# Expert retrieval of a two-layer decoder on one core: selection of pairs in calls of four heads over 64 candidates, tile 2's keys chosen within the up pass, gate groups from tile 53

## The chip, the cores and the metric

The kernel runs on 1 core of one Trainium2 chip. Its time is the device time of one execution in microseconds (us), the median over runs. TensorE is written PE, its weight load PEld, VectorE DVE, ScalarE ACT, GpSimd POOL, and SyncE, which only issues transfers here, SP.

## The reference, cut to what matters

The model is one step of a decoder with two layers, for 512 prompt tokens and 64 sample tokens. Each layer ends with a channel mixer (PEER) that is nearly all of the time:

```
def peer(xn, wq, subkeys, u, v):                      # 8 heads, 16 of 128 x 128 experts a head
    q = (xt @ wq).reshape(t, 8, 2, 128)
    s = einsum('thpc,pnc->thpn', q, subkeys)          # 2 x 128 scores a head
    sv, si = top_k(s, 16)
    cand = sv[:, :, 0, :, None] + sv[:, :, 1, None, :]      # 16 x 16 sums
    cv, ci = top_k(cand.reshape(t, 8, 256), 16)
    ia, ib = si[..0..][ci // 16], si[..1..][ci % 16];  eidx = ia * 128 + ib
    gate = softmax(cv)
    hc = gelu(einsum('chkd,cd->chk', u[eidx], x), approximate=False)
    return einsum('chk,chkd->cd', hc * gate, v[eidx])
```

Since both lists of 16 are sorted, a sum at place (i, j) can be among the 16 largest only if (i+1)(j+1) is at most 16. 50 of the 256 places are such.

## The kernel before, in words

The 576 tokens are four tiles of 128 prompt tokens (0 to 3) and 64 sample tokens. The mixer treats them in two ways. **Dense:** for the 384 tokens of tiles 0 to 2 every one of the 16384 experts is computed, 128 experts at a time: the *up pass* of 128 expert tiles `m` (`up(m)`: 24 matmuls of 128x384, results through Gelu to HBM), then the *down pass* of 128 tiles (`down(n)`), where the hidden values are weighed with a gate matrix that is zero for experts not chosen. The gate matrix is made during the up pass, four tokens at a time (a *group*, 96 a layer): DVE makes one-hot vectors (`one_hots`, tiles hotA and hotB), ACT weighs them (`weigh_ones`), PE multiplies them (`gates`), ACT copies the result (`copy_gates`), and eight groups are stored in one 2 MB transfer. **Sparse:** for the 64 sample tokens and tile 3 the chosen rows of `u` and `v` are gathered from HBM by POOL, 128 rows of 4 KB at once (`gather(k)`, 192 gathers of `u` a layer), and DVE forms a dot product of each (`dots`, tiles rowsA and rowsB, a ring of 8 slots: gather k waits for dot k-8).

Matmuls in float32 are done in three passes on a rounded half and a rest: ACT makes `high` of each expert tile (`high_tile`), POOL makes `low` (L490), PE needs both.

Ahead of the up pass, PE projects 16 query tiles (`project_tile`) and scores each against the keys (`scores(j)`, j = 0 to 15: head j//2, side j%2), ACT copies the scores (`copy_scores`), and DVE selects. `stage1(l, j)` takes the 16 best of 128 keys for four token tiles (`max`, `max_index`, `match_replace`, `max`, `max_index`). `stage1_samples` does the same for the samples, `best_pairs` selects 16 pairs from 16 x 16 sums and looks up their two indices with one-hot compares, products and sums of 16 x 16 elements a pair list. It is called for one head at a time of tile 3 (`last_tile_pairs`, 8 calls) and of the samples (`sample_pairs`, 4 calls of two heads folded on the partitions) while the queries are made, and for eight heads of tiles 0 to 2 (`dense_pairs`) during the up pass. The gathers wait for `picked`, which follows the sparse selections.

All order is written by hand, and every engine executes its list in order. Three schedules tie the engines together by the expert tile m of the up pass:

- POOL issues `low(m)` and then gathers until `gathers_by(m)` of them are issued, so `low(m+1)` stands behind the gathers of m.
- ACT, after the Gelu of tile m, executes `weigh_ones` of the groups of tile m+1, `copy_gates` of the groups of m, and then `high_tile(m + 3)`. `groups_of(m)` is set by GROUP0 (first tile with a group) and GROUPS_PER_TILE.
- DVE executes the three `dense_pairs` with 20 dots in each, then the dots up to 64, then `one_hots`: before group g stand 64 + 7/5 g dots (two after each of two groups in five, one after the others). DVE can be at most six groups ahead of PE.

Of the kernel before, what the change touches and what calls it, by code (L numbers as in the profile page):

```python
# [25 lines left out]
P = 128  # L26
# [26 lines left out]

C_ID, C_IOTA, C_FOLD = 0, P, 2 * P
# [42 lines left out]
EXP_S, EXP_T = 8, (14, 26, 39)  # L97
TURN_T = (28, 41, 52)
GROUP0, GROUPS_PER_TILE = 45, 1.25
# [13 lines left out]
def gathers_by(m):  # L113

    if m < 4:
        n = 0
    elif m < 6:
        n = 4 * (m - 3)
    elif m < GROUP0:
        n = 8 + 1.55 * (m - 5)  # L120
    else:
        n = 70 + 1.7 * (m - GROUP0)
    return min(int(n), DOTS_UP + 3)
# [6 lines left out]
    "sc_read": 2 * PH, "scS_read": PH // 2, "ss_done": PH // 2, "ex_in": PH + PH // 2 + ND, "ex_out": 2 + ND, "turned": ND, "slot_ready": ND, "slots": ND,  # L130
# [43 lines left out]
def decoder(nc, xin, consts, params, wts, wv, stconv, kcT, kc, vc, uT, u, v,  # L174
            yT, convP, hOut, kNew, vNewP, vNewS, kKeep, vKeep, convS, gate_dram, s_dram):
    with ExitStack() as ctx:
# [90 lines left out]
        cabf = st.take("cabf", [P, 2, PH, TOPK])  # L267
# [9 lines left out]
        sc = st.take("sc", [P, 6, 4, KEYS])  # L277
        sc2 = st.take("sc2", [P, 4, KEYS])
        scS2 = st.take("scS2", [P, 2, KEYS])
        qT = st.take("qT", [P, 6, T])  # L280
        st = Span(nc, gblk_at, SB_HI)
# [224 lines left out]
        def _(act):  # L506
# [70 lines left out]
            def queries(l):  # L577
                d0 = (D_PQ0, D_PQ1)[l]

                def copy_scores(j):  # L580
                    act.wait_ge(sem("sc_done"), after("sc_done", l, j + 1))
                    if j >= 6:
                        act.wait_ge(sem("sc_read"), after("sc_read", l, j - 5))
                    act.activation(sc[:, j % 6].rearrange("p t k -> p (t k)"), ps[:, 4 + j % 2, :], ACT.Copy
                                   ).then_inc(sem("sc_copied"), 1)
# [27 lines left out]
            def hidden(l):  # L613
# [34 lines left out]
                for m in range(KEYS):  # L648
# [119 lines left out]
        def _(dve):  # L768
# [125 lines left out]
            def stage1(l, j):  # L894

                b = sc[:, j % 6]
                dve.wait_ge(sem("sc_copied"), after("sc_copied", l, j + 1))
                for t in range(4):
                    chain.did(dve.max(sv[:, t, j, 0:8], b[:, t]))
                chain.settle()  # L900
                for t in range(4):
                    chain.did(dve.max_index(si[:, t, j, 0:8], sv[:, t, j, 0:8], b[:, t]))  # L902
                    chain.did(dve.match_replace(sc2[:, t], sv[:, t, j, 0:8], b[:, t], BIG))
                chain.settle()
                for t in range(4):
                    ins = dve.max(sv[:, t, j, 8:16], sc2[:, t])
                    if t < 3:
                        chain.did(ins)
                ins.then_inc(sem("sc_read"), 1)
                chain.settle()  # L910
                dve.wait_ge(sem("sc_read"), after("sc_read", l, j + 1))
                for t in range(4):
                    chain.did(dve.max_index(si[:, t, j, 8:16], sv[:, t, j, 8:16], sc2[:, t]))  # L913
# [22 lines left out]
            def experts(l):  # L936
# [36 lines left out]
                def best_pairs(svt, sit, nh, g, ex, ia, ib, free=None, between=None):  # L973


                    c, c2 = cand[:, 0:nh], cand2[:, 0:nh]
# [5 lines left out]
                    chain.did(dve.tensor_tensor(  # L982
                        c.rearrange("p h (i j) -> p h i j", i=TOPK),
                        s4[:, :, 0].unsqueeze(3).broadcast_to([P, nh, TOPK, TOPK]),
                        sb.unsqueeze(2).broadcast_to([P, nh, TOPK, TOPK]), ALU.add))
# [28 lines left out]
                    chain.did(dve.tensor_scalar(cab[:, 0, 0:nh], ci[:, 0:nh], 4, None, ALU.logical_shift_right))  # L1014
                    chain.did(dve.tensor_scalar(cab[:, 1, 0:nh], ci[:, 0:nh], TOPK - 1, None, ALU.bitwise_and))
# [6 lines left out]
                    eq = [b_.rearrange("p h (k i) -> p h k i", k=TOPK) for b_ in (c, c2)]  # L1022
# [294 lines left out]
        def _(pe):  # L1317
# [42 lines left out]
            def experts(l):  # L1360
                w0, d0 = (W_PQ0, W_PQ1)[l], (D_PQ0, D_PQ1)[l]

                def scores(j):
# [4 lines left out]
                    for t in range(4):  # L1368
                        ins = pe.matmul(ps[:, 4 + j % 2, t * KEYS:(t + 1) * KEYS], qT[:, j % 6, t * P:(t + 1) * P], sk,
# [314 lines left out]
```

## Time and profile before

| | |
|---|---|
| median of 3 runs | 3456.17 us (3449.89 to 3461.92) |
| the profiled execution | 3455.42 us, its span 3453.6 us |
| busy: PE, PEld, DVE, ACT, POOL | 89%, 81%, 75%, 40%, 47% of the span |
| DMA | 927 MB, 268 GB/s over the span |
| chain that ended last | PE 61%, DVE 25%, DMA 8% |

A layer's mixer goes through the query stage (from 299 us in layer 0, from 2039 us in layer 1), the up pass (to 1125 and 2864 us) and the down pass (538 us each). The share of an engine says little here, for the three stages have different limits; windows and the steps of one tile tell more. A busy PE is modelled: it counts as busy when its matmuls are merely stretched.

### The profile page before, as it was taken

How to read it: one execution, taken by the hardware profiler on the slowest of the kernel's cores; microseconds unless marked ns; L12 is line 12 of the kernel's file. 1: busy time of each engine (PE TensorE's matmuls, PEld its weight loads, DVE VectorE, ACT ScalarE, POOL GpSimd, SP SyncE). 2: the span in 40 equal slices, each digit the busy share in tenths (PEclk: the TensorE clock that was granted, in tenths of full speed). 3: DMA queues.
4: the chain of work that ended last, by engine and by line, in shares of the span. 5: the costliest groups of instructions: out<-in, count | busy, mean ns of one | idle time of the engine just before them, and what ended most of it. 6: DMA issues, size and time to landing. Idle time of an engine off the chain costs nothing.

```text
span 3453.6 us, 46653 instructions
## 1 busy us (share of the span) xinstructions
PE 3077.7 (89%) x17142; PEld 2786.4 (81%) x17142; DVE 2603.6 (75%) x5039; ACT 1373.3 (40%) x2513; POOL 1620.5 (47%) x1157
## 2 busy tenths in 40 slices
PE   6865959999999899999787789499999998999996
PEld 5765959999999688888684679499999997888885
DVE  3745999976653799999657349899766646999997
ACT  2312214466665233333334222144666653333332
POOL 3441239877776234333230032299777763333340
PEclk9977979999999999999897799799999999999998
DMA  3354239999998999999220022299999989999993
GB/s 96 97 26 56 65 127 362 349 360 374 343 347 307 377 412 404 412 410 406 99 74 18 7 61 63 87 344 361 369 359 367 337 311 381 409 405 411 409 410 129
DMA packets 297411, 927.21 MB, mean 268 GB/s; under 512 B 36640, under 2 KB 86560, under 8 KB 293392
## 3 DMA queue, kind: packets, MB, share of 16 engines
q1 hardware_dynamic: 164016, 418.78, 35.2%
q0 software_dynamic: 111280, 404.77, 31.0%
q10 hardware_dynamic: 21888, 100.67, 7.2%
q8 instruction: 137, 2.24, 0.3%
q14 instruction: 90, 0.74, 0.1%
HBM read 820.48 MB, written 105.53 MB: 268 GB/s over the span
## 4 chain that ended last, share of the span: by engine, by line
PE 61%; DVE 25%; DMA 8%; issue 2%; ACT 2%; POOL 2%; SPq 0%; DVEq 0%; ACTq 0%; POOLq 0%
PE ps L1442 31%; PE ps L1390 14%; PE ps L1340 8%; PE ps L1422 4%; DMA rowsB<-u,pick 3%; DVE rowsB L959 2%; DVE rowsA L959 2%; POOL low L490 1%; DMA hOut<-hlast 1%; DMA sring<-s_dram 1%; DVE cand L1024 1%; DVE cand L1031 1%; DVE si L913 1%; DVE si L902 1%; DMA rowsA<-u,pick 1%
## 5 line engine op out<-in xcount | busy, mean ns | idle before, releaser
L611 ACT ACTIVATE high<-raw 128x1024 fp32r<-128x1024 f32 x512 | 541.9, 1058 | 918.4 <-PE ps L1442 686.6
L1390 PE MATMUL ps<-xh,high 128*128 128x384 f32 x2048 | 706.7, 345 | 60.3 <-POOL low L490 60.1
L490 POOL TENSOR_TENSOR low<-raw,high 128x1024 fp32r<-128x1024 f32 x256 | 613.8, 2398 | 255.6 <-ACT high L611 252.7
L1390 PE MATMUL ps<-xh,low 128*128 128x384 f32 x2048 | 690.6, 337 | 0.0
L1390 PE MATMUL ps<-xl,high 128*128 128x384 f32 x2048 | 689.7, 337 | 0.0
L1442 PE MATMUL ps<-high,hh 128*128 128x512 f32 x1536 | 483.8, 395 | 27.0 <-DVE low L1103 27.0
L1442 PE MATMUL ps<-low,hh 128*128 128x512 f32 x1536 | 482.0, 395 | 0.0
L1442 PE MATMUL ps<-high,hl 128*128 128x512 f32 x1536 | 480.7, 394 | 0.0
L1390 PEld LDWEIGHTS ps<-xh,high 128*128 128x128 f32 x2048 | 389.2, 190 | 68.3 <-POOL low L490 66.5
L1390 PEld LDWEIGHTS ps<-xl,high 128*128 128x128 f32 x2048 | 389.3, 190 | 0.0
L1390 PEld LDWEIGHTS ps<-xh,low 128*128 128x128 f32 x2048 | 388.0, 189 | 0.0
L481 POOL DMA_INDIRECT rowsB<-v,pick x192 | 200.2, 1043 | 365.2 <-DVE ps L966 313.7
L959 DVE SCALAR_TENSOR_TENSOR rowsB<-rowsB,ps 128x1024 f32<-128x1024 f32 x192 | 232.4, 1214 | 182.3 <-DMA rowsB<-u,pick 181.7
L1442 PEld LDWEIGHTS ps<-high,hh 128*128 128x128 f32 x1536 | 288.7, 188 | 95.5 <-DVE low L1103 27.7
L481 POOL DMA_INDIRECT rowsA<-v,pick x192 | 196.6, 1024 | 318.3 <-DVE ps L966 312.2
L1442 PEld LDWEIGHTS ps<-low,hh 128*128 128x128 f32 x1536 | 288.4, 188 | 70.9
L1442 PEld LDWEIGHTS ps<-high,hl 128*128 128x128 f32 x1536 | 289.0, 188 | 69.3
L1340 PE MATMUL ps<-xh,high 128*128 128x288 f32 x1184 | 266.9, 308 | 81.6 <-DVE xl L788 81.5
L959 DVE SCALAR_TENSOR_TENSOR rowsA<-rowsA,ps 128x1024 f32<-128x1024 f32 x192 | 231.9, 1213 | 107.9 <-DMA rowsA<-u,pick 107.2
L1103 DVE TENSOR_TENSOR low<-raw,high 128x1024 fp32r<-128x1024 f32 x256 | 311.6, 1217 | 0.0
L630 ACT ACTIVATE hotB<-hotB,slotT 128x128 f32<-128x128 f32 x768 | 242.0, 390 | 76.3 <-DVE hotB L1078 75.9
L653 ACT ACTIVATE sring<-ps 128x384 f32<-128x384 f32 x256 | 124.7, 487 | 367.6 <-PE ps L1390 366.5
(234 smaller groups left out, 5190.0 us busy)
## 6 DMA issues: line engine op xcount, KB each, us to landing
raw<-uT SPq DMA_DIRECT2D x256, 512.0 KB, 6.9
raw<-v SPq DMA_DIRECT2D x256, 512.0 KB, 10.3
s_dram<-sring ACTq DMA_DIRECT2D x128, 384.0 KB, 7.1
gate_dram<-gblk ACTq DMA_DIRECT2D x24, 2048.0 KB, 11.1
gt<-gate_dram SPq DMA_DIRECT2D x32, 1536.0 KB, 15.8
sring<-s_dram SPq DMA_DIRECT2D x128, 384.0 KB, 10.6
raw<-wts SPq DMA_DIRECT2D x76, 512.0 KB, 3.6
rowsB<-u,pick POOLq DMA_INDIRECT x192, 8.2
```

Source lines behind the costliest of these rows:

```text
L481: pool.indirect_dma_start(out=row_slot(k), out_offset=None, in_=u if k < S0 + S1 else v, in_offset=bass.IndirectOffsetOnAxis(ap=pick[:, c: ...
L490: pool.tensor_tensor(low[:, m % 4], raw[:, m % 4], high[:, (m + 2) % 3].bitcast(F32), ALU.subtract).then_inc(sem("lo_ready"), 1)
L611: act.activation(high[:, (m + 2) % 3], tile_raw(m), ACT.Copy).then_inc(sem("hi_ready"), 1)
L630: ins = act.activation(hotB[:, k], hotB[:, k], ACT.Copy, scale=slotT[:, 2, n:n + 1])
L653: act.activation(sring[:, p % 4, m % 2], ps[:, m % 2, 0:DN], ACT.Gelu).then_inc(sem("g_up"), 1)
L902: chain.did(dve.max_index(si[:, t, j, 0:8], sv[:, t, j, 0:8], b[:, t]))
L959: dve.scalar_tensor_tensor(row, row, 1.0, wide(XS0 if k < S0 else XS1), ALU.mult, ALU.mult, accum_out=phid[:, c:c + 1]).then_inc(sem("row_ ...
L1103: dve.tensor_tensor(tile_low(m), tile_raw(m), high[:, (m + 2) % 3].bitcast(F32), ALU.subtract).then_inc(sem("vlo_ready"), 1)
L1340: ins = pe.matmul(ps[:, 2 * i + h, 0:H2], a[:, c], x[:, c, h * H2:(h + 1) * H2], start=(c == 0 and j == 0), stop=(c == NC - 1 and j == 2))
L1390: ins = pe.matmul(ps[:, m % 2, 0:DN], w[:, c], x[:, c, 0:DN], start=(c == 0 and k == 0), stop=(c == NC - 1 and k == 2))
L1422: ins = pe.matmul(ps[:, 2 + g % 2, i * P:(i + 1) * P], hotB[:, k], hotA[:, k], start=True, stop=True)
L1442: ins = pe.matmul(ps[:, YC[c] + d, :], h[:, n % 3, c * P:(c + 1) * P], w[:, d * 512:(d + 1) * 512], start=(n == 0 and i == 0), stop=(n == ...
```

## The change

It has four parts. (1) `best_pairs` forms only 64 sums (rows of 16, three of 8, four of 4, eight of 1: PAIR_ROWS) instead of 256, scans 64 elements, and turns the place in the list of 64 into i and j with a chain of 14 small instructions. It is called for four heads at once: twice for tile 3 and once for the samples. (2) `stage1` treats token tiles 0, 1 and 3 only. Tile 2's scores are kept (scL) and selected by `stage1_late` between `dense_pairs(1)` and `dense_pairs(2)`, 16 lists in four lots, each lot followed by two dots. The ring of score copies is 4 deep instead of 6. (3) `gathers_by` starts at tile 7 instead of 4, and runs at 1.45 a tile instead of 1.55, then at 1.95 instead of 1.7. (4) Groups begin at tile 53 instead of 45, at 1.4 a tile instead of 1.25. Exponentials and transposes of the slots move to later tiles.

```diff
-EXP_S, EXP_T = 8, (14, 26, 39)
-TURN_T = (28, 41, 52)
-GROUP0, GROUPS_PER_TILE = 45, 1.25
+EXP_S, EXP_T = 12, (22, 34, 54)
+TURN_T = (32, 52, 66)
+GROUP0, GROUPS_PER_TILE = 53, 1.4
+SCR = 4
+EARLY, LATE = (0, 1, 3), 2
...
 def gathers_by(m):
-    if m < 4:
+    if m < 7:
         n = 0
-    elif m < 6:
-        n = 4 * (m - 3)
+    elif m < 9:
+        n = 4 * (m - 6)
     elif m < GROUP0:
-        n = 8 + 1.55 * (m - 5)
+        n = 8 + 1.45 * (m - 8)
     else:
-        n = 70 + 1.7 * (m - GROUP0)
+        n = 74 + 1.95 * (m - GROUP0)
     return min(int(n), DOTS_UP + 3)
...
+            def stage1_late(js):
+                chain.settle()
+                for j in js:
+                    chain.did(dve.max(sv[:, LATE, j, 0:8], scL[:, j]))
...
                 def best_pairs(svt, sit, nh, g, ex, ia, ib, free=None, between=None):
-                    c, c2 = cand[:, 0:nh], cand2[:, 0:nh]
+                    c, c2 = cand[:, 0:nh, 0:PAIRS], cand2[:, 0:nh, 0:PAIRS]
...
-                    for a in range(2):
-                        chain.did(dve.tensor_copy(cabf[:, a, 0:nh], cab[:, a, 0:nh]))
+                    chain.did(dve.tensor_copy(i_, cab[:, 0, 0:nh]))
+                    chain.did(dve.tensor_copy(j_, cab[:, 1, 0:nh]))
+                    chain.settle()
+                    dots(g)
+                    chain.did(dve.tensor_scalar(i_, i_, -1.0, 0.0, ALU.add, ALU.max))
+                    chain.settle()
+                    chain.did(dve.scalar_tensor_tensor(i_, j_, -6.0, i_, ALU.add, ALU.max))
...
                 for j in range(2 * PH):
                     stage1(l, j)
-                    if j % 2:
-                        chain.settle()
-                        last_tile_pairs(j // 2)
                     if j % 4 == 0 and j:
-                        sample_pairs(j // 4 - 1)
-                sample_pairs(PH // 2 - 1)
+                        stage1_samples(l, j // 4 - 1)
+                    if j == PH:
+                        last_tile_pairs(0)
+                stage1_samples(l, PH // 2 - 1)
+                sample_pairs()
                 take_rows(0, S0, slot[:, 0, 0, 0:S0], slot[:, 0, 1, 0:S0])
+                last_tile_pairs(1)
                 take_rows(S0, S1, slot[:, 1, 0], slot[:, 1, 1])
                 dense_pairs(0, normalise_sparse)
                 dense_pairs(1, lambda: normalise_dense(0))
+                for q in range(4):
+                    stage1_late(range(4 * q, 4 * q + 4))
+                    dots(2)
                 dense_pairs(2, lambda: normalise_dense(1))
```

On DVE, in `best_pairs` for eight heads of a dense tile, the piece from the last scans to the first one-hot compare was this before (cab and cabf hold the split place, the row with rowsA or rowsB is a dot):

```order
L1010 MAX_INDEX ci_101<-cv_100,cand2_105 128x8 x2
L959 SCALAR_TENSOR_TENSOR rowsA_118,phid_89<-rowsA_118,ps 128x1024
L1014 TENSOR_SCALAR cab_102<-ci_101 128x128
L1015 TENSOR_SCALAR cab_102<-ci_101 128x128
L1018 CAST cabf_103<-cab_102 128x128 x2
L1024 TENSOR_TENSOR cand_104<-cabf_103,ps 128x2048
```

and is this in the changed kernel:

```order
L1043 TENSOR_SCALAR cab_102<-ci_101 128x128
L1044 TENSOR_SCALAR cab_102<-ci_101 128x128
L1045 CAST cabf_103<-ci_101 128x128
L1047 CAST cabf_103<-cab_102 128x128
L1048 CAST cabf_103<-cab_102 128x128
L982 SCALAR_TENSOR_TENSOR rowsA_119,phid_89<-rowsA_119,ps 128x1024
L1051 TENSOR_SCALAR cabf_103<-cabf_103 128x128
L1053 SCALAR_TENSOR_TENSOR cabf_103<-cabf_103 128x128
L1055 SCALAR_TENSOR_TENSOR cabf_103<-cabf_103 128x128
L1057 TENSOR_SCALAR cabf_103<-cabf_103 128x128
L1058 TENSOR_SCALAR cabf_103<-cabf_103 128x128
L1060 SCALAR_TENSOR_TENSOR cabf_103<-cabf_103 128x128
```

Four small instructions became fourteen (two TENSOR_TENSOR follow the rows shown after one more SCALAR_TENSOR_TENSOR), nearly all with SBUF operands alone, and one dot stands between them: a dense call holds 21 dots instead of 20.

On DVE, at the first gate group, the list before was (the x4 row is `dots(S0 - rows_done)`; 64 dots stand ahead of the first hotA):

```order
L1037 TENSOR_REDUCE slot_94<-cand2_105 128x128
L959 SCALAR_TENSOR_TENSOR rowsB_88,phid_89<-rowsB_88,ps 128x1024
L959 SCALAR_TENSOR_TENSOR rowsA_118,phid_89<-rowsA_118,ps 128x1024 x4
L1078 TENSOR_TENSOR hotA_107<-ps,slotT_93 128x512
L1078 TENSOR_TENSOR hotB_108<-ps,slotT_93 128x512
L959 SCALAR_TENSOR_TENSOR rowsB_88,phid_89<-rowsB_88,ps 128x1024 x2
```

and is now:

```order
L1084 TENSOR_REDUCE slot_94<-cand2_105 128x128
L982 SCALAR_TENSOR_TENSOR rowsA_119,phid_89<-rowsA_119,ps 128x1024
L1125 TENSOR_TENSOR hotA_107<-ps,slotT_93 128x512
L1125 TENSOR_TENSOR hotB_108<-ps,slotT_93 128x512
L982 SCALAR_TENSOR_TENSOR rowsA_119,phid_89<-rowsA_119,ps 128x1024
L982 SCALAR_TENSOR_TENSOR rowsB_88,phid_89<-rowsB_88,ps 128x1024
```

71 dots (3 x 21 + 8) stand ahead of the first group now. On POOL, from the low half of tile 44, the list before was (one row of L490 is a tile's low half, the DMA rows behind it are its gathers):

```order
L490 TENSOR_TENSOR low<-raw,high 128x1024
L481 DMA rowsB<-u,pick 128x1024 x2
L490 TENSOR_TENSOR low<-raw,high 128x1024
L481 DMA rowsA<-u,pick 128x1024 x2
L490 TENSOR_TENSOR low<-raw,high 128x1024
L481 DMA rowsA<-u,pick 128x1024
```

and from the low half of tile 52 it is now:

```order
L498 TENSOR_TENSOR low<-raw,high 128x1024
L489 DMA rowsA<-u,pick 128x1024
L498 TENSOR_TENSOR low<-raw,high 128x1024
L489 DMA rowsA<-u,pick 128x1024
L489 DMA rowsB<-u,pick 128x1024 x2
L498 TENSOR_TENSOR low<-raw,high 128x1024
L489 DMA rowsB<-u,pick 128x1024
```

Up to tile 45, where the first group belonged, 70 gathers were issued before; up to tile 53, where it belongs now, 74.

## Rows read from the trace of the kernel before

**Rows 1.** Windows of layer 0: bounds, length, busy (count) by engine, PEclk, DMA, GB/s

```profile
299.00:421.00 122.00, 113.70 (x841) 112.36 (x842) 104.97 (x511) 32.58 (x47) 33.54 (x14) 0.93 0.19 59
421.00:493.00 72.00, 38.89 (x257) 37.62 (x256) 68.15 (x351) 14.43 (x19) 12.28 (x6) 0.78 0.22 66
507.00:674.00 167.00, 165.51 (x943) 162.55 (x942) 166.35 (x355) 71.19 (x92) 150.28 (x100) 1.00 0.98 355
674.00:886.00 212.00, 211.14 (x1356) 211.03 (x1356) 151.47 (x255) 141.02 (x332) 164.70 (x112) 1.00 0.97 362
886.00:1083.00 197.00, 185.02 (x1154) 183.34 (x1153) 118.31 (x198) 118.81 (x278) 134.27 (x91) 0.97 0.91 337
```

**Rows 2.** Timeline of POOL, layer 0, the first gather (start, length, what, idle before it)

```profile
492.57 1.10 POOL L481 DMA_INDIRECT rowsB<-u,pick  x1 [33.71 <-DVE pick L1045]
```

**Rows 3.** Timeline of DVE in the query stage of layer 0

```profile
347.58 0.18 DVE L979 COPY ps<-sv 128x16 f32<-128x16 f32 x1
...
353.72 0.87 DVE L899 MAX8 sv<-sc 128x8 f32<-128x128 f32 x4
...
358.88 0.48 DVE L922 MAX8 svS<-ps 128x8 f32<-128x128 f32 x2
...
361.78 0.18 DVE L979 COPY ps<-svS 128x16 f32<-128x16 f32 x1
```

**Rows 4.** Timeline of DVE in the first dense call of layer 0

```profile
505.82 1.40 DVE L988 MAX8 cv<-cand 128x8 f32<-128x256 f32 x4
507.13 1.20 DVE L959 SCALAR_TENSOR_TENSOR rowsB<-rowsB,ps 128x1024 f32<-128x1024 f32 x1
...
508.26 0.09 DVE L993 MATCH_VALUE_LOAD ci<-cv,cand 128x8 f32 x1
...
509.06 0.08 DVE L993 MATCH_VALUE_LOAD ci<-cv,cand 128x8 f32 x1
```

**Rows 5.** Timeline at 376 us, query stage, POOL and DVE

```profile
376.62 2.39 POOL L461 TENSOR_TENSOR low<-raw,high 128x1024 fp32r<-128x1024 f32 x1 [5.67 <-ACT high L526]
376.70 2.41 DVE L1018 CAST cabf<-cab 128x16 f32<-128x16 uint32 x2
```

**Rows 6.** Timeline of DVE: second and third dense call, first gate group

```profile
558.80 0.42 DVE L980 CAST ps<-si 128x256 f32<-128x256 uint32 x1
...
615.38 0.42 DVE L980 CAST ps<-si 128x256 f32<-128x256 uint32 x1
...
676.34 0.68 DVE L1078 TENSOR_TENSOR hotB<-ps,slotT 128x512 f32<-128x512 f32 x1
```

**Rows 7.** Timeline of layer 0 from the low half of tile 91 to that of tile 94

```profile
912.42 2.42 POOL L490 TENSOR_TENSOR low<-raw,high 128x1024 fp32r<-128x1024 f32 x1
...
914.99 0.95 POOL L481 DMA_INDIRECT rowsB<-u,pick  x1 [0.16 <-issue]
...
927.92 1.22 DVE L959 SCALAR_TENSOR_TENSOR rowsB<-rowsB,ps 128x1024 f32<-128x1024 f32 x1 [5.05 <-DMA rowsB<-u,pick]
...
930.38 0.40 ACT L630 ACTIVATE hotB<-hotB,slotT 128x128 f32<-128x128 f32 x1 [6.08 <-DVE hotB L1078]
...
933.17 2.38 POOL L490 TENSOR_TENSOR low<-raw,high 128x1024 fp32r<-128x1024 f32 x1 [6.68 <-ACT high L611]
```

**Rows 8.** POOL, layer 0: low halves of tiles 98 and 116

```profile
953.70 2.36 POOL L490 TENSOR_TENSOR low<-raw,high 128x1024 fp32r<-128x1024 f32 x1 [1.50 <-ACT high L611]
...
1060.34 2.39 POOL L490 TENSOR_TENSOR low<-raw,high 128x1024 fp32r<-128x1024 f32 x1 [0.73 <-ACT high L611]
```

**Rows 9.** The page's DMA issues (us from issue to landing, median)

```profile
rowsB<-u,pick POOLq DMA_INDIRECT x192, 8.2
```

**Rows 10.** The chain that ended last, from 844 us (start, length, what)

```profile
849.89 4.18 PE ps L1390 x24
854.06 0.89 PE ps L1422 x8
```

More of the change, by code:

```diff
@@ L51 @@
 BIG = -3.0e38
+PAIR_ROWS = ((0, 1, 16), (1, 3, 8), (4, 4, 4), (8, 8, 1))
+PAIRS = sum(n * w for _, n, w in PAIR_ROWS)
 C_ID, C_IOTA, C_FOLD = 0, P, 2 * P
@@ L266, in decoder @@
         cab = st.take("cab", [P, 2, PH, TOPK], U32)
-        cabf = st.take("cabf", [P, 2, PH, TOPK])
+        cabf = st.take("cabf", [P, 5, PH, TOPK])
         cand = st.take("cand", [P, PH, TOPK * TOPK])
@@ L276, in decoder @@
         st = Span(nc, gblk_at, SB_HI)
-        sc = st.take("sc", [P, 6, 4, KEYS])
+        sc = st.take("sc", [P, SCR, 3, KEYS])
         sc2 = st.take("sc2", [P, 4, KEYS])
@@ L280, in decoder @@
         qT = st.take("qT", [P, 6, T])
+        scL = st.take("scL", [P, 2 * PH, KEYS])
         st = Span(nc, gblk_at, SB_HI)
@@ L581, in copy_scores @@
                     act.wait_ge(sem("sc_done"), after("sc_done", l, j + 1))
[L582 to L585, printed above, removed]
+                    if j >= SCR:
+                        act.wait_ge(sem("sc_read"), after("sc_read", l, j - SCR + 1))
+                    n = len(EARLY) * KEYS
+                    act.activation(sc[:, j % SCR].rearrange("p t k -> p (t k)"), ps[:, 4 + j % 2, 0:n], ACT.Copy)
+                    act.activation(scL[:, j], ps[:, 4 + j % 2, n:], ACT.Copy).then_inc(sem("sc_copied"), 1)
                 for f in range(2 * PH):
@@ L894, in stage1 @@
             def stage1(l, j):
-                b = sc[:, j % 6]
+                b = sc[:, j % SCR]
                 dve.wait_ge(sem("sc_copied"), after("sc_copied", l, j + 1))
-                for t in range(4):
-                    chain.did(dve.max(sv[:, t, j, 0:8], b[:, t]))
+                for i, t in enumerate(EARLY):
+                    chain.did(dve.max(sv[:, t, j, 0:8], b[:, i]))
                 chain.settle()
-                for t in range(4):
-                    chain.did(dve.max_index(si[:, t, j, 0:8], sv[:, t, j, 0:8], b[:, t]))
-                    chain.did(dve.match_replace(sc2[:, t], sv[:, t, j, 0:8], b[:, t], BIG))
+                for i, t in enumerate(EARLY):
+                    chain.did(dve.max_index(si[:, t, j, 0:8], sv[:, t, j, 0:8], b[:, i]))
+                    chain.did(dve.match_replace(sc2[:, i], sv[:, t, j, 0:8], b[:, i], BIG))
@@ L904, in stage1 @@
                 chain.settle()
[L905 to L909, printed above, removed]
-                chain.settle()
-                dve.wait_ge(sem("sc_read"), after("sc_read", l, j + 1))
-                for t in range(4):
-                    chain.did(dve.max_index(si[:, t, j, 8:16], sv[:, t, j, 8:16], sc2[:, t]))
+                dve.memset(mark[:, :], 0.0).then_inc(sem("sc_read"), 1)
@@ new lines, in stage1 @@
+                for i, t in enumerate(EARLY):
+                    chain.did(dve.max(sv[:, t, j, 8:16], sc2[:, i]))
+                chain.settle()
+                for i, t in enumerate(EARLY):
+                    chain.did(dve.max_index(si[:, t, j, 8:16], sv[:, t, j, 8:16], sc2[:, i]))
+            def stage1_late(js):
[3 more added lines that the diff above has]
+                chain.settle()
+                for i, j in enumerate(js):
+                    chain.did(dve.max_index(si[:, LATE, j, 0:8], sv[:, LATE, j, 0:8], scL[:, j]))
+                    chain.did(dve.match_replace(sc2[:, i], sv[:, LATE, j, 0:8], scL[:, j], BIG))
+                chain.settle()
+                for i, j in enumerate(js):
+                    chain.did(dve.max(sv[:, LATE, j, 8:16], sc2[:, i]))
+                chain.settle()
+                for i, j in enumerate(js):
+                    chain.did(dve.max_index(si[:, LATE, j, 8:16], sv[:, LATE, j, 8:16], sc2[:, i]))
+                chain.settle()
@@ L981, in best_pairs @@
                     chain.settle()
[L982 to L985, printed above, removed]
+                    at = 0
+                    for i, n, w in PAIR_ROWS:
+                        chain.did(dve.tensor_tensor(
+                            c[:, :, at:at + n * w].rearrange("p h (i j) -> p h i j", j=w),
+                            s4[:, :, 0, i:i + n].unsqueeze(3).broadcast_to([P, nh, n, w]),
+                            sb[:, :, 0:w].unsqueeze(2).broadcast_to([P, nh, n, w]), ALU.add))
+                        at += n * w
                     chain.settle()
```

48 lines of the change are left out of this document (31 added, 17 removed).

## The prediction, made before the change was run

> **What bounds the kernel now.** I read the windows first, then the chain, the waits of the up pass, and the timelines of DVE, POOL and ACT tile by tile. In the query stage DVE is nearly full (105.0 of 122 us, then 68.2 of 72) while PE falls to 38.9 of 72 us [rows 1]: the 12 one-head selections and the last lists hold up `picked`, and POOL, which has the first gather at the head of its list, stands idle 33.7 us until 492.57 [rows 2]. PE cannot go past the tiles whose low halves are made. From 507 to 674 us POOL is busy 150 of 167 us, DVE 166, PE 165.5 [rows 1]: nothing is lost but the pace of POOL and DVE. From 674 to 886 PE runs without a hole: 4.2 us for a tile and 0.9 for a group [rows 10]. From 886 to 1083 PE has holes of 12 us in 197 [rows 1]. The rest is the down pass, which the change leaves alone.
>
> The holes after 886 are a loop. A tile's gather is issued behind its low half (914.99 after 912.42), its row lands 12.9 us later, DVE makes the dot and the next one-hots (927.92), ACT had waited 6.1 us for them (930.38), then makes the high half of a tile three further on, and POOL its low half at 933.17 after a wait of 6.7 us [rows 7]. The loop is 2.6 + landing + 2.5 + 2.8 = 7.9 us and the landing, whose median is 8.2 us [rows 9]: about 16 us for a gather that is first behind its low half, 1.3 more for a second one (a gather issue of 0.95 and its gap). How many tiles the loop may take follows from the schedules: group g needs 64 + 7g/5 dots, the tile where `gathers_by` reaches that number is known, and the low half that waits is that of the weighing tile plus three. In the kernel before this distance is 5 tiles for the first groups, 4 for groups 21 to 48, 3 from about group 66 (tile 98). Four tiles take PE 21 us, more than the loop; three take 15.9 (3 x 4.2 and 3.75 x 0.9), which is not. There the tiles are loop-paced: from the low half of 98 to that of 116, six times round, 106.6 us, 17.8 a round [rows 8].
>
> **The change part by part, layer 0.** *Query stage.* `stage1` of four tiles takes 5.16 us, the samples' 2.90, a one-head selection 6.14 [rows 3]. Three tiles: three quarters and a settled wait, 4.05. A scan of 256 elements starts every 0.33 us (1.31 for four), one of 128 every 0.20 (0.87 for four, less the last one's tail) [rows 3, 4]; 64 elements are not in the trace. By the same slope 0.13; it cannot be over 0.20, nor under the 0.06 that the slope leaves at zero. A call of four heads is then 6 operations of 1024 elements (1.13 each by the slope), 20 scans and the rest: 14.4 us, and some waits for POOL (below). So DVE loses 12 x 6.14 and 16 x 1.1 and gains three calls of 16: 43 us less ahead of the dense calls. It now needs 4.75 us a query tile, and PE, 841 instructions in 113.7 us [rows 1], 0.135 each and 920 for the stage, 7.8: PE bounds the queries, and the first tile-3 call hides in what DVE has to spare. Last scores on DVE at 433; `stage1` and samples to 440; `sample_pairs` with POOL beside it 18; `picked` at 459 instead of 492; second tile-3 call to 475. POOL gathers up to 8 meanwhile and then waits for the first dot at 476, which costs PE a few us at tiles 9 to 12 (tile 12 ends at about 492). The shorter ring of score copies costs nothing while DVE keeps up; 4 tiles are 31 us against a lag of 16.
>
> *Tiles 12 to 52.* 1.45 gathers a tile bring POOL under PE, so PE goes at 4.2: tile 52 ends at 660. DVE: a dense call took 56.6 us from the second to the third [rows 6]. Removed: 40 scans by 0.20 and 1.4 of the sums, 9.3; added: ten small instructions with waits 2.5, a dot 1.1 (507.13 to 508.26) [rows 4]. The small ones have SBUF operands alone. A cast issued at 376.70 beside POOL's low half of 376.62 ended with it, 2.4 us later for 0.25 us of work [rows 5]. POOL is in such an operation more than half of the time here, so a chain of 3.4 us meets one or two: 5 us of waiting instead of 1.5. Between no meeting and four, a call costs 0 to 9.6 more; I take 3.5, as the gap between two low halves holds about six of the instructions. A call: 54.4. Three are 163, the late lists 16 x 1.2 and settled waits 21, their 8 dots 9, one wait for an exponential 1.5: one-hots of group 0 at 475 + 195 + 1.3 = 672, against 677.0 before [rows 6]. The Trainium skill (SBUF — State Buffer, "SBUF: two separate sides") says the pair of ports that DVE and GpSimd share is held for a whole instruction, also by a DVE operation with two SBUF inputs. By that rule the new chain waits as taken here; the cast of [rows 5] agrees, and no wait would bring 672 to 661.
>
> So the same moment that had gates for tile 45 has them for tile 53, and tile 53 waits some 12 us for them. In matmuls this is 8 tiles or 33 us less to do, and 5 us earlier.
>
> *Gate part.* Here the schedules have changed against the loop. 71 dots stand ahead of group 0 and 74 gathers belong to tile 53: a lead of 3 rows instead of 6, and 1.95 / 1.4 rows a group do not raise it against 1.4 dots. Counted with the same rule, the distance is 3 tiles for most groups from the first, and 2 for 23 of them (groups 3, 6, 7, 13, 17, ... 83), until the dots end at group 86. A tile now needs PE 4.2 + 1.4 x 0.9 = 5.4 us, so two tiles are 10.9 and three 16.3, against rounds of 16 to 18. A round of two tiles cannot be absorbed, since the next one starts from the late tile. The path with most rounds from tile 55 to 117 has 24 (10 of two tiles, 14 of three). All two-tile rounds hang on a first gather: 16.0. For the others I take the 17.8 measured [rows 8]. 10 x 16.0 + 14 x 17.8 = 409 us for 62 tiles, 6.6 a tile.
>
> **The sum.** Low half of tile 55 at 672 + 2.8 (weighing to low half, [rows 7]) = 675, that of 117 at 1084. Before, that of 116 came at 1060.3, so 117 at 1065.4 [rows 8]: 18.4 later. Off it 5, because a loop-paced low half is used at once where one on time lies some 5 us ahead (15.2 for three tiles less 4.2, 0.5, 2.8 and 2.6), and on it one group, 0.9. 14 us a layer, 29 in all; layer 1 goes through the same stages. Against the profiled execution's 3455.4 us: **3484 us**. The median of the runs shown is 0.8 above it, which changes nothing.
>
> **The rivals.** *The loop does not close* (0.14). Early groups may run ahead on stored slack, so PE or the bytes bound the gate part. A tile moves 0.52 (raw) + 1.95 x 0.52 + 0.20 + 1.4 x 0.26 = 2.11 MB; at the 362 GB/s of 674 to 886 [rows 1] 5.8 us. 62 tiles 361 instead of 409: tile 117 at 1036, 34 us a layer earlier with the corrections: 3388. For it: PE has no hole between 674 and 886, where the loop also ran [rows 1]. Against: that was with distances of 4 and 5.
> The Trainium skill (DMA: Bandwidth & Descriptors, "Specifications") gives 358 GB/s from HBM to a core. By that the tile is 5.9 us and the time would be some 9 us above this rival's; the trace shows 355 to 362 in these stages, so it neither adds nor forbids.
> *Shorter rounds and no waits for POOL* (0.22): landings near 8 all along and DVE early, 24 x 16 = 384 from 664: tile 117 at 1051, 19 a layer earlier, 3418. It turns slower to faster where rounds average under 16.4 us.
> *Longer rounds* (0.09): more rows a tile lengthen landings, 18.5 a round, 444 from 675: 3555.
> *The stage ahead gains nothing that lasts, loop as before* (0.05): 3456.
> The forecast itself 0.50, from 3450 to 3520.
>
> **How the numbers follow.** A difference under 0.3% (10 us) cannot be told from none. Faster: both faster rivals but for a little of the second, and a small edge of the forecast, 0.34. Same: an edge of the forecast, the fifth case, 0.13. Slower 0.53. The range 3395 to 3545 leaves out most of the first rival and half of the fourth, and holds the bounds of the scans (8 us a layer) and of the chain.
>
> **What would show it.** First gather near 459 us, first group near 672 with PE waiting at tile 53. Then steps of 6.5 us a tile, DVE waiting for rows and ACT for hotB from tile 55 on, PE holes of 50 us and more up to tile 115. Wrong if ACT hardly waits for hotB: then the rows came early enough. Wrong too if dense calls take over 60 us or under 50, or if PE already waits for POOL between tiles 12 and 52.

## The result, and the profile after

The changed kernel takes 3519.03 us, median of 4 runs (3517.71 to 3531.53), against 3453.03 of the kernel before (4 runs, 3445.74 to 3461.92). The ratio is 1.0198, 95% interval 1.0174 to 1.0221: slower by 2.0%, where 3484 us, 0.8% slower, was forecast. The profiled execution took 3517.74 us with a span of 3515.9.

Windows of the changed kernel, layer 0 (columns as in [rows 1]: bounds, length, busy of PE, PEld, DVE, ACT, POOL, granted clock, DMA share, GB/s):

```profile
299.00:421.00 122.00, 120.22 (x908) 119.14 (x909) 84.47 (x450) 36.53 (x66) 35.93 (x15) 0.97 0.22 66
421.00:461.00 40.00, 40.00 (x258) 39.29 (x257) 38.66 (x193) 15.24 (x22) 22.80 (x12) 1.00 0.50 150
491.00:668.00 177.00, 169.83 (x960) 166.87 (x959) 171.41 (x470) 68.75 (x90) 150.66 (x98) 0.99 0.94 335
668.00:684.00 16.00, 5.36 (x29) 5.04 (x28) 16.00 (x20) 2.95 (x7) 5.18 (x5) 0.70 0.59 217
684.00:900.00 216.00, 187.38 (x1141) 184.57 (x1140) 132.73 (x223) 126.25 (x300) 138.85 (x97) 0.94 0.84 311
900.00:1098.00 198.00, 170.90 (x1035) 169.12 (x1034) 118.60 (x200) 111.04 (x264) 124.82 (x88) 0.94 0.85 309
```

Against [rows 1]: PE is full from 299 to 461 us, where it had been busy 38.9 of 72 us from 421 on, so the query stage is PE's now. At 668 to 684 it stands and waits for the first group. Then come 414 us in which it is never full: busy 358 of them, at a mean granted clock of 0.94, where the kernel before had 211 of 212 us at 1.00 from 674 to 886.

The page's costliest groups (busy, mean ns | idle ahead of them, who ended most of it), both layers:

```profile
L498 POOL TENSOR_TENSOR low<-raw,high 128x1024 fp32r<-128x1024 f32 x256 | 613.4, 2397 | 377.1 <-ACT high L620 374.2
L639 ACT ACTIVATE hotB<-hotB,slotT 128x128 f32<-128x128 f32 x768 | 243.3, 391 | 251.3 <-DVE hotB L1125 250.9
L1471 PE MATMUL ps<-hotA,hotB 128*128 128x128 f32 x1536 | 214.5, 288 | 125.3 <-ACT gblk L647 100.2
```

ACT waits 251 us for one-hots. PE does not wait for low halves, as the forecast had it, but in front of its gates. Its waits from 684 to 1098 us (who, on what: sum, times, longest):

```profile
PE ps L1471 <- ACT gblk L647: 53.8, 20, 7.1
PE ps L1471 <- ACT hotB L639: 1.9, 2, 1.3
```

Three places on POOL, which answer to [rows 2, 8]: the first gather, and the low halves of tiles 55 and 117.

```profile
453.97 1.05 POOL L489 DMA_INDIRECT rowsB<-u,pick  x1 [0.60 <-DVE pick L1092]
...
683.73 2.38 POOL L498 TENSOR_TENSOR low<-raw,high 128x1024 fp32r<-128x1024 f32 x1 [10.34 <-ACT high L620]
...
1097.50 2.37 POOL L498 TENSOR_TENSOR low<-raw,high 128x1024 fp32r<-128x1024 f32 x1 [0.36 <-ACT high L620]
```

The gather of 492.57 is issued at 453.97. The two low halves are 413.8 us apart, 6.67 a tile. In the kernel before the same two stand at 719.9 and 1065.4, 5.57 a tile. So the changed kernel enters the gate part 36 us ahead and leaves it 32 us behind. One round of the row loop that takes two tiles, from the low half of tile 107 to that of 109 (POOL, DVE, ACT and PE in order of time):

```profile
1032.86 2.39 POOL L498 TENSOR_TENSOR low<-raw,high 128x1024 fp32r<-128x1024 f32 x1 [5.76 <-ACT high L620]
1035.39 0.96 POOL L489 DMA_INDIRECT rowsB<-u,pick  x1
...
1043.23 1.22 DVE L982 SCALAR_TENSOR_TENSOR rowsB<-rowsB,ps 128x1024 f32<-128x1024 f32 x1 [7.38 <-DMA rowsB<-u,pick]
...
1044.98 0.68 DVE L1125 TENSOR_TENSOR hotB<-ps,slotT 128x512 f32<-128x512 f32 x1
...
1045.69 1.28 ACT L639 ACTIVATE hotB<-hotB,slotT 128x128 f32<-128x128 f32 x4 [5.14 <-DVE hotB L1125]
1046.88 0.57 ACT L647 ACTIVATE gblk<-ps 128x512 f32<-128x512 f32 x1
...
1047.35 1.04 ACT L620 ACTIVATE high<-raw 128x1024 fp32r<-128x1024 f32 x1
...
1048.48 2.40 POOL L498 TENSOR_TENSOR low<-raw,high 128x1024 fp32r<-128x1024 f32 x1 [6.11 <-ACT high L620]
```

```profile
1047.60 1.13 PE L1471 MATMUL ps<-hotA,hotB 128*128 128x128 f32 x8 [2.78 <-ACT gblk L647]
```

Every link is the forecast's: gather behind the low half, 7.8 us to the landing, dot, one-hots, weighing, high half, low half, 15.6 us in all. What the forecast left out is a side branch. ACT copies the gates behind the weighing, and PE, which has two banks for gates, waits 2.78 us for that copy at once, without the detour over the low half.

### The profile page after: what moved, and what is told of

Read it like the earlier page. It is cut to its first block, busy times and chain, and to the rows that moved or that the text cites. A ratio compares the mean times of both kernels' runs of the same rounds, so it can differ in the third digit from the quotient of the medians.

```text
span 3515.9 us, 46591 instructions
## 1 busy us (share of the span) xinstructions
PE 3114.0 (89%) x17142; PEld 2818.3 (80%) x17142; DVE 2550.5 (73%) x4975; ACT 1375.9 (39%) x2545; POOL 1619.6 (46%) x1157
## 4 chain that ended last, share of the span: by engine, by line
PE 49%; DVE 21%; DMA 14%; POOL 7%; ACT 5%; issue 3%; SPq 0%; ACTq 0%; DVEq 0%; POOLq 0%
PE ps L1491 31%; PE ps L1389 10%; DMA rowsB<-u,pick 6%; POOL low L498 5%; DMA rowsA<-u,pick 5%; PE ps L1439 4%; DVE rowsB L982 2%; DVE rowsA L982 2%; ACT hotB L639 1%; ACT high L620 1%; DMA hOut<-hlast 1%; DMA sring<-s_dram 1%; DVE cand L1071 1%; DVE cand L1078 1%; DVE slot L1084 1%
## 5 line engine op out<-in xcount | busy, mean ns | idle before, releaser
L620 ACT ACTIVATE high<-raw 128x1024 fp32r<-128x1024 f32 x512 | 541.7, 1058 | 881.8 <-PE ps L1491 686.7
L1439 PE MATMUL ps<-xh,high 128*128 128x384 f32 x2048 | 716.9, 350 | 23.0 <-POOL low L498 22.8
L1439 PE MATMUL ps<-xh,low 128*128 128x384 f32 x2048 | 700.2, 342 | 0.0
L1439 PE MATMUL ps<-xl,high 128*128 128x384 f32 x2048 | 700.1, 342 | 0.0
L1439 PEld LDWEIGHTS ps<-xh,high 128*128 128x128 f32 x2048 | 398.3, 194 | 30.1 <-POOL low L498 29.2
L1439 PEld LDWEIGHTS ps<-xl,high 128*128 128x128 f32 x2048 | 397.4, 194 | 0.0
L1439 PEld LDWEIGHTS ps<-xh,low 128*128 128x128 f32 x2048 | 395.8, 193 | 0.0
L1471 PE MATMUL ps<-hotA,hotB 128*128 128x128 f32 x1536 | 214.5, 288 | 125.3 <-ACT gblk L647 100.2
```

Source lines behind the costliest of these rows:

```text
L620: act.activation(high[:, (m + 2) % 3], tile_raw(m), ACT.Copy).then_inc(sem("hi_ready"), 1)
L1439: ins = pe.matmul(ps[:, m % 2, 0:DN], w[:, c], x[:, c, 0:DN], start=(c == 0 and k == 0), stop=(c == NC - 1 and k == 2))
L1471: ins = pe.matmul(ps[:, 2 + g % 2, i * P:(i + 1) * P], hotB[:, k], hotA[:, k], start=True, stop=True)
```

## The experiments

Theory: the lead of the gathers over the dots (74 against 71) closes the row loop at two or three tiles, and this paces the gate part. Rivals: landings and bytes at 1.95 rows and 1.4 groups a tile; or the new selection itself. Times below are medians, ratios are to the kernel before, with a 95% interval; beside these runs the kernel before took 3452 to 3457 us, so the times can be set against each other to some 5 us.

### The lead alone: 77, 75, 73 and 76

```
     else:                                   # the same rule, only from tile 54 on
-        n = 74 + 1.95 * (m - GROUP0)
+        n = 77 + 1.95 * (m - GROUP0)        # 75, 76; 73 from tile 53 on
```

> The changed kernel, with gathers_by at 77 + 1.95 a tile instead of 74 + 1.95 from tile 54 on, and nothing else changed: the rows are asked for three earlier against the dots. Theory (row loop): counted with the same rule, the distance that a row loop may take becomes 4 or 5 tiles for nearly all groups, 22 us or more of PE work against rounds of 16 to 18, so the loop no longer sets the pace of the gate part. It then goes at the bytes' 5.8 us a tile instead of 6.67, low half of tile 117 near 1045 us instead of 1097.5, some 50 us a layer, 3415 us (3390 to 3445), faster than both kernels. Rival 1 (what paces the gate part is 1.95 rows and 1.4 groups a tile, by landings or bytes, not the lead): steps stay at 6.4 us or more, 3490 to 3520. Rival 2 (the loss is made ahead of tile 53, by the selection): the gate part hardly moves, 3510 to 3520.

> As the run before, with 75 + 1.95: one row earlier than in the changed kernel. Row loop: distances 3 (65 groups) and 4 (23), none of 2. Three tiles take PE 16.4 us against rounds of 16 to 17.8, so 5.8 to 6.0 us a tile: tile 117 near 1050, 3425 us (3400 to 3460). The step from 74 to 75 should be worth much more than all steps from 75 to 77. Rival 1: no change, 3490 to 3520. If the lead helps in proportion instead of by whole tiles, a third of what 77 gives.

> The other way: 73 + 1.95 from tile 53, one row later than in the changed kernel. Row loop: distance 2 for 67 groups instead of 23. Rounds of 15.5 to 16 us for two tiles most of the time, over 7 us a tile: tile 117 60 to 75 us a layer later than in the changed kernel, 3650 us (3620 to 3680). Rivals 1 and 2: within 10 us of 3519.

> As lead 77 and lead 75, with 76 + 1.95. Measured so far, layer 0, low half of tile 55 to that of 117: 7.57 us a tile at 73, 6.67 at 74, 6.03 at 75, 5.43 at 77, where PE's own work is the limit. Row loop in whole tiles: at 76 the distance is 4 for 65 groups and 3 for 22, four tiles are 21.7 us of PE work against a round of 17 to 18, so only the 22 short ones can hold PE up, and what they lose is regained by the slack of the others only in part: 5.45 to 5.6 a tile, 3370 us (3360 to 3385). If the pace follows the lead evenly it lies in the middle between 75 and 77: 5.73 a tile, 3405 us.

| lead rule | us a tile, low half 55 to 117, layer 0 / 1 | time, us | ratio |
|---|---|---|---|
| 73 | 7.57 / 7.62 | 3634.88 | 1.0527 (1.0490 to 1.0563) |
| 74 (the change) | 6.67 / 6.63 | 3519.03 | 1.0198 (1.0174 to 1.0221) |
| 75 | 6.05 / 6.06 | 3445.83 | 0.9973 (0.9956 to 0.9989) |
| 76 | 5.70 / 5.66 | 3393.96 | 0.9824 (0.9795 to 0.9852) |
| 77 | 5.43 / 5.44 | 3364.89 | 0.9749 (0.9712 to 0.9786) |

One integer of the schedule moves the time by 270 us. Windows with a lead of 77:

```profile
684.00:850.00 166.00, 166.00 (x1074) 165.96 (x1073) 121.88 (x210) 116.03 (x275) 129.67 (x91) 1.00 0.97 370
850.00:1018.00 168.00, 168.00 (x1091) 168.00 (x1090) 125.29 (x212) 118.43 (x282) 128.74 (x89) 1.00 1.00 391
```

and with 73:

```profile
684.00:850.00 166.00, 134.05 (x788) 131.37 (x788) 91.59 (x156) 88.26 (x208) 93.54 (x66) 0.90 0.76 270
850.00:1018.00 168.00, 133.91 (x775) 130.64 (x774) 85.75 (x145) 82.69 (x196) 93.72 (x66) 0.89 0.77 276
```

With 77 PE has no hole and does a tile in its own 5.4 us, with as many rows and groups a tile as before. Both rivals fall: neither bytes (391 GB/s are moved here) nor the selection sets this pace. The expected 5.8 us a tile by bytes made the forecast of 3415 us 50 too slow. 73 and 75 came out within their ranges, but not the order of the steps: from 74 to 75 the time falls by 73 us and from 75 to 77 by 81, where the first step was to be worth much more.

76 was the test of the counting rule. Whole tiles gave 3370 us, an even dependence 3405 and 5.73 us a tile; measured are 3394 and 5.70. (The pace at 75, 6.03 in that expectation, is 6.05 by the low halves of 680.1 and 1055.0.) The time lies outside the range of 3360 to 3385, and the pace nearer the even dependence. So the counting in whole tiles is too sharp: short rounds cost something even when most are long. The steps, 116, 73, 52 and 29 us for one row each, get smaller towards PE's own pace.

### Schedule and selection apart

The kernel before with its own selection and the new groups, at a lead of 3 and of 6 rows over its 64 dots; the kernel before with only its gather rule changed (its two numbers, offset and pace, though the expectation calls them one); and the new selection with the old groups:

```
-TURN_T = (28, 41, 52)                       # before's selection, new schedule
-GROUP0, GROUPS_PER_TILE = 45, 1.25
+TURN_T = (28, 41, 66)
+GROUP0, GROUPS_PER_TILE = 53, 1.4
...
-        n = 8 + 1.55 * (m - 5)
+        n = min(8 + 1.55 * (m - 5), 66)     # 69
-        n = 70 + 1.7 * (m - GROUP0)
+        n = 67 + 1.95 * (m - GROUP0)        # 70
```

> The kernel before with its own selection (256 candidates, one head at a time, tile 2 with the others), but with groups from tile 53 at 1.4 a tile, and gathers at 67 + 1.95 from tile 53 (held at 66 up to it): a lead of 3 rows over its 64 dots, as the changed kernel has over its 71. The last transpose of the slots moves from tile 52 to 66. Row loop: up to tile 53 nothing waits, PE is there near 707 us; from there the gate part goes as in the changed kernel, 6.67 us a tile, low half of 117 near 1125, end of the up pass near 1183 instead of 1125, 57 us a layer slower than the kernel before, 3565 us (3530 to 3590). Rival 2 (the new selection makes the loss): this one is not slower than the kernel before, 3420 to 3460.

> The kernel before's own selection with groups from tile 53 at 1.4 a tile, and now the lead that lead 77 has: gathers at 70 + 1.95 over its 64 dots (held at 69 up to tile 53), last transpose at 66. Row loop: no wait from 681 us on, tile 53 near 707, then 5.43 us a tile (337 us for 62 tiles, as with 77): low half of 117 near 1048, end of the up pass near 1107 instead of 1125, 18 us a layer faster than the kernel before: 3418 us (3400 to 3440). Against lead 77 (3365) it then shows what the new selection is worth with the same schedule: some 50 us. If the new selection were worth nothing, it would be at 3365.

```
-        n = 70 + 1.7 * (m - GROUP0)         # the kernel before
+        n = 71 + 1.75 * (m - GROUP0)
```

> The kernel before, with one number changed: gathers at 71 + 1.75 a tile instead of 70 + 1.7 from tile 45 on. If its holes after 886 us are the row loop closing at three tiles, as the forecast read them (106.6 us from tile 98 to 116 where PE's work takes 95), they go: the distance stays at 4 or 5 to the end, the up pass ends near 1109 to 1112 instead of 1125, 3424 us (3415 to 3435). If those holes are something else (bytes at 362 GB/s, landings), within 10 us of 3454.

```
-GROUP0, GROUPS_PER_TILE = 53, 1.4           # the changed kernel
+GROUP0, GROUPS_PER_TILE = 45, 1.25
-EXP_S, EXP_T = 12, (22, 34, 54)
+EXP_S, EXP_T = 12, (22, 34, 44)
-        n = 8 + 1.45 * (m - 8)
+        n = 8 + 1.7 * (m - 8)
-        n = 74 + 1.95 * (m - GROUP0)
+        n = 77 + 1.7 * (m - GROUP0)
```

> The changed kernel's selection (64 candidates, four heads, tile 2 late) with groups from tile 45 at 1.25 a tile and the lead of the kernel before: gathers at 77 + 1.7 over 71 dots (1.7 a tile up to tile 45); the third exponential at 44. Row loop: the first group cannot come before some 678 us whatever the schedule, so PE stands at tile 45 from 635 to there, and then everything goes as in the kernel before: end of the up pass 1127 (before 1125), 3455 us (3440 to 3470). The whole gain of the earlier queries is then lost at tile 45, and only a later first group can keep it. If the selection itself were what makes the changed kernel slow, this one would be as slow: 3500 or more.

| | old selection | new selection |
|---|---|---|
| groups from 45 at 1.25 | 3453 (as it was) | 3463.54, 1.0017 (1.0003 to 1.0031) |
| groups from 53 at 1.4, lead 3 | 3592.99, 1.0399 (1.0364 to 1.0433) | 3519.03, 1.0198 |
| groups from 53 at 1.4, lead 6 | 3418.80, 0.9891 (0.9871 to 0.9911) | 3364.89, 0.9749 |

The new selection is worth 74 and 54 us where the groups begin at 53 and nothing where they begin at 45: there PE, which comes earlier to its first gates, waits 20.6 us in one piece for the first one-hots, and the up pass of layer 0 ends at 1131.8, 6 us after that of the kernel before. The lead of 3 costs 174 us with the one and 154 with the other. The kernel before with 71 + 1.75 takes 3423.62 us (0.9905, 0.9888 to 0.9921; forecast 3424), and its window that answers to the last of [rows 1] has no hole left:

```profile
886.00:1083.00 197.00, 197.00 (x1269) 197.00 (x1269) 118.16 (x198) 131.95 (x313) 142.54 (x94) 1.00 0.94 356
```

The old selection with the lead of 6 is as expected (3418). With the lead of 3 it came out 28 us above its expectation: 6.77 us a tile, and 65.6 us instead of 60 from the low half of 117 to the Gelu of 127. Counted by the schedule its last rows are asked for at tile 118, those of the changed kernel at 114, so the loop goes on past the low half of 117; no run tests that.

### The chain of small instructions in PSUM

```
-                    i_, j_, q_, t_, t2_ = (cabf[:, a, 0:nh] for a in range(5))
+                    is_, j_, q_, t_, t2_ = (cabf[:, a, 0:nh] for a in range(5))
+                    i_ = by_head(sbP[:, 0:nh * TOPK])
...
                     chain.did(dve.tensor_tensor(t_, t_, t2_, ALU.min))
+                    chain.did(dve.tensor_copy(is_, i_))
```

> The changed kernel, with the running value i of the chain of small instructions held in PSUM (where the copied scores were) and copied to SBUF at its end: four of the chain's instructions with two SBUF inputs have one now, two keep two. The schedule is the changed kernel's. If waits for POOL's low halves make the first dense call longer than the forecast's 54.4 us (it took 63.1, and its chain held four instructions of 1.4 to 3.1 us for 0.15 to 0.3 of work), then these four instructions no longer stretch; the casts and the last two may. First group's one-hots some 5 us earlier than 680.9, the gate part the same 414 us from then: 3509 us (3500 to 3518). If the stretches are something else (a settled wait, the scan ahead), they stay and the time is 3519.

DVE in the first dense call of the changed kernel, and two of POOL's low halves beside it. A duration of 3 us is a wait inside the instruction, for work of 0.3:

```profile
500.25 1.50 DVE L1043 TENSOR_SCALAR cab<-ci 128x128 uint32<-128x128 uint32 x1
...
502.24 3.04 DVE L1048 CAST cabf<-cab 128x128 f32<-128x128 uint32 x1
...
506.72 0.29 DVE L1053 SCALAR_TENSOR_TENSOR cabf<-cabf 128x128 f32<-128x128 f32 x1
507.05 3.08 DVE L1055 SCALAR_TENSOR_TENSOR cabf<-cabf 128x128 f32<-128x128 f32 x1
...
510.56 3.12 DVE L1060 SCALAR_TENSOR_TENSOR cabf<-cabf 128x128 f32<-128x128 f32 x1
```

```profile
507.55 2.42 POOL L498 TENSOR_TENSOR low<-raw,high 128x1024 fp32r<-128x1024 f32 x1
...
511.10 2.41 POOL L498 TENSOR_TENSOR low<-raw,high 128x1024 fp32r<-128x1024 f32 x1
```

The two long DVE instructions, of 507.05 and 510.56, end 0.16 and 0.17 us after these two low halves. So it is with all eleven small instructions that are stretched in the three calls of layer 0, eight of them in the chain and three in the normalisation: each ends 0.09 to 0.17 us after a low half.

The same piece with i in PSUM:

```profile
498.40 2.98 DVE L1049 CAST cabf<-cab 128x128 f32<-128x128 uint32 x1
...
503.22 0.30 DVE L1056 SCALAR_TENSOR_TENSOR ps<-cabf,ps 128x128 f32<-128x128 f32 x1
...
504.07 0.29 DVE L1061 SCALAR_TENSOR_TENSOR cabf<-ps,cabf 128x128 f32<-128x128 f32 x1
...
504.60 1.64 DVE L1064 TENSOR_TENSOR cabf<-cabf 128x128 f32<-128x128 f32 x1
```

In three calls none of the instructions with a PSUM input was stretched; those that kept SBUF operands alone still were. Counted from the first Gelu of the layer, the first one-hots end after 246.9 and 244.5 us instead of 252.3 and 250.8. The time is 3506.61 us, 1.0150 (1.0126 to 1.0175), as expected (3509); the two ratios' intervals just touch, so the traces carry more than the time. The Trainium skill (SBUF — State Buffer, "SBUF: two separate sides") says that a DVE operation with two SBUF inputs, or one in a two-port performance mode, contends with GpSimd for a pair of ports as a whole, one waiting for the other's end. The runs agree for operations with two SBUF inputs. The TENSOR_SCALAR of 1.50 us and the CAST of 3.04 have one input, in SBUF, and wait too; whether they ran in such a mode the trace does not show.

### A later first group

```
-GROUP0, GROUPS_PER_TILE = 53, 1.4           # lead 77; gathers held at 74 up to GROUP0
+GROUP0, GROUPS_PER_TILE = 56, 1.4           # then 56, 1.47 (rows 2.06 a tile),
                                             # then 55, 1.44 (2.02) with i in PSUM
```

> Lead 77, with the first group three tiles later, at tile 56 (gathers held at 74 up to it, then 77 + 1.95 a tile from there). PE waited some 14 us at tile 53 for the first group; three tiles are 12.6 us of work that it can do there. Then 5.43 us a tile with groups as before: end of the up pass some 12 us a layer earlier, 3341 us (3333 to 3352). If another wait takes its place at once (gates copied, bytes, rows), nothing: 3365.

> Lead 77 with the first group at tile 56 as in the run before it (3359 us), and now 1.47 groups and 2.06 rows a tile, so that the last group falls at tile 121 as with groups from 53, not 124. In that run PE had gained 11.3 us by the low half of tile 117 and lost 14 after it: the last gate block was stored only at 1058 to 1064 us, SP had waited for it with the first loads of v, ACT waited 9.0 and 6.7 us for them ahead of the Gelus of tiles 126 and 127. If that is the cause, the loss goes: end of the up pass some 12 us a layer before lead 77's, 3341 us (3333 to 3350). If the loss comes from the late end of the rows or of the DMA bytes, it stays: 3355 to 3365.

> Lead 77, the chain's i in PSUM as in the run with that (first group 671.3 instead of 681.0), first group at tile 55, at 1.44 groups and 2.02 rows a tile: last group at tile 121. PE is at the gates of tile 55 near 677, the first group is ready by 673: nothing is waited for there, PE works from 491 us to the down pass but for some us between tiles 12 and 52. End of the up pass 14 us a layer before lead 77's: 3337 us (3328 to 3348). If the earlier first group is worth nothing once the groups begin later, it ends with the run before, within 5 us.

Groups from 56 at 1.4: 3359.42 us, 0.9717 (0.9696 to 0.9737), a miss. ACT at the end of the up pass:

```profile
1058.07 0.33 ACTq L655 DMA_DIRECT2D gate_dram<-gblk  x1
...
1071.12 1.06 ACT L622 ACTIVATE high<-raw 128x1024 fp32r<-128x1024 f32 x1 [9.02 <-DMA raw<-v]
1072.09 0.47 ACT L664 ACTIVATE sring<-ps 128x384 f32<-128x384 f32 x1
...
1079.22 1.06 ACT L622 ACTIVATE high<-raw 128x1024 fp32r<-128x1024 f32 x1 [6.66 <-DMA raw<-v]
```

The last gate block is stored at 1058 us, SP issues the first loads of v only behind it, and the high halves of v stand ahead of the Gelus of 126 and 127. With the last group at tile 121 again these waits are gone (low half of 117 to Gelu 127: 59.7 us, 73.5 in the run before it), but the time is 3353.47 us, 0.9704 (0.9687 to 0.9720), a second miss. The profiled execution came to the Gelu of tile 52 at 670.6 us, 9.2 after that of lead 77 with the same code ahead of it, and the gate part took 5.51 a tile. All four executions lie between 3350 and 3355 us, so this was no single late one; the cause stays open. With i in PSUM and groups from 55 it is 3334.76 us, 0.9660 (0.9643 to 0.9677), as expected (3337), the fastest of all and 3.4% faster than the kernel before. It differs from the run before it in three things at once (PSUM, first group, pace), so no share of the 19 us between them belongs to one of them for certain:

```profile
684.00:1000.00 316.00, 315.38 (x2053) 315.02 (x2052) 239.25 (x407) 221.66 (x534) 247.32 (x172) 1.00 1.00 392
```

## Why the prediction was right in direction and wrong in size

**Right.** PE bounds the query stage, the first gather comes early (453.97; 459 forecast), PE waits at tile 53 for the first group, and the row loop sets the pace of the gate part, with 55.7 us of waits of PE (50 and more forecast). That term, 409 us from the low half of tile 55 to that of 117, measured 413.8. The lead runs, the two-by-two table and the kernel before with a new gather rule show the loop by taking it away. Inside the term the sizes were off both ways: the 23 two-tile rounds that the trace has took 12.0 to 19.3 us, mean 14.9 instead of 16.0. With ten of them in the sum, the fourteen longer rounds come to some 18.9 instead of 17.8. The two errors nearly cancel, so that 409 lies this close to 413.8 is in part luck. One cause of the first is the landing, for which the forecast took the median of the whole run, 8.2 us: for rows issued from 684 to 1098 us it is 6.5 (rowsA) and 7.2 (rowsB) in the changed kernel. The 76 run shows that "two or three tiles" is a coarse measure of a lead that acts row by row.

**Wrong, the step that failed.** The sum for a layer: 31.8 us measured in layer 0 and 28.1 in layer 1, 14.3 forecast. Of the 17.5 that lack in layer 0, 12.7 are in the two terms around the gate part:
- "A call: 54.4", and with it "one-hots of group 0 at ... 672". The three dense calls took 63.1, 53.5 and 56.7 us, 173.3 instead of 163.2; the first is over the 60 that the forecast had named as a sign of being wrong. Its chain waited some 9.7 us for POOL's low halves where 5 were taken (the 3.5 beyond the 1.5 of before). Over the three calls the chain's waits are 18.5 against 15, so they are 3.5 of the 10.1. The rest is not shown by a run; the trace has in these calls three stretched normalisations (1.19, 2.08 and 2.03 us), a wait of 1.7 for an exponential and 3.3 for rows. (The scans of 64 elements take 0.14 us, 0.13 forecast.) First one-hots end at 681.0, and the low half of 55 comes at 683.7 instead of 674.8: 8.9 us. The forecast's terms themselves add up to 671.3, not 672.
- "Off it 5, because a loop-paced low half is used at once". Next to nothing is to be taken off. From the low half of 117 to the Gelu of 127 it is 60.0 us in the kernel before, 59.7 in the changed one, 59.7 with lead 77, where nothing is loop-paced: ACT makes the high half behind a Gelu, which ties the low half to the tile in all three. (With a lead of 73 and with i in PSUM it is 57.4 in layer 0, so up to 2.6 can come off.) PE's waits in the loop are for gate copies (53.8 us), next to none for low halves. Forecast were 5 off and 0.9 on, measured is 0.3 off: 3.8 us.
- The rest, 4.8, is the gate part.

The largest of these is the first. The PSUM run takes 5 to 6 us a layer of it away, as waits for POOL: in layer 0 the first one-hots end at 671.3 us, and at 671.2 in the other run with i in PSUM, while in the seven executions with the old chain and the same code up to tile 53 they end between 677.4 and 687.9. The second is read from the traces alone, from the same two instructions in three kernels.

**The rivals.** "The loop does not close" with its bytes at 362 GB/s was ruled out, and its price was wrong too: without the loop a tile takes 5.43 us, not 5.8. In "shorter rounds and no waits for POOL" the two-tile rounds were shorter, but the waits for POOL were longer than forecast; and its sum is wrong, for 384 from 664 is 1048, not 1051, some 3412 us instead of 3418. "Longer rounds" by longer landings is contradicted by the landings of 6.5 and 7.2 us.

## What to carry to other kernels

When a schedule lets a consumer's work begin later and run denser, count again how far each producer's request stands ahead of its use, in units of the round trip: here asking for the rows one place earlier was worth 29 to 116 us, and the rebuilt selection 54 to 74. Vary that integer first, in both directions; it changes one line, and its slope tells whether the loop is what binds. And an early stage that gets faster pays only if the next hand-over is moved with it (3464 against 3365 us).

## What the runs showed of the hardware

- **A wait of PE costs more than itself.** From the low half of 55 to that of 117 the changed kernel takes 413.8 us and lead 77 336.7, 77 more, but PE waits only 55.7 of them. In the other 21 PE is busy, 358 us for what takes 337: the mean granted clock is 0.94 there, between the levels of 1.2 and 2.4 GHz, and 1.00 with lead 77; with a lead of 73 it is 0.90 and 0.89. Of what a hole costs, a good quarter does not show among the waits.
- **DMA moves more than the up pass of before showed.** It moves 391 GB/s over 168 us and 392 over 316. So 355 to 362 was no limit. The trace of the kernel before showed that already, in its down pass, which the forecast did not use (columns as in [rows 1]):

```profile
1139.00:1677.00 538.00, 537.67 (x2304) 433.12 (x2304) 499.13 (x576) 184.43 (x252) 191.76 (x184) 1.00 0.98 384
```

The Trainium skill (DMA: Bandwidth & Descriptors, "Specifications") gives 358 GB/s from HBM to a core; these windows lie above it. Rows land later when more is moved: for those issued from 684 us on in the gate part of layer 0 the median from issue to landing is 5.7 to 6.2 us with a lead of 73 (270 to 276 GB/s), 6.5 to 7.2 in the changed kernel (309 to 311), 8.1 to 8.5 with 77 (370 to 391) and 9.0 to 10.3 in the fastest kernel (392).
- **DVE's waits for POOL vary from execution to execution.** With the same code up to tile 53, the first dense call of layer 0 took 63.1 us in the changed kernel, 58.7, 58.4 and 66.4 with leads of 77, 75 and 73. The stretched instructions of its chain account for some 9.7, 5.3, 5.0 and 13.2 us of these; without them the call is 53.3 to 53.5 us in all four. A price taken from one call of one profile is good to some 4 us.
